# The layout of a pair of activation halves, and the rounding of buffer addresses, in a two-block transformer kernel

## The reference

```python
h = rmsnorm(x, norm_mix_g)
u = h @ w_in                                  # 1024 -> 5376
x = x + merged(rwkv(u), diff_attention(u)) @ w_out
h = rmsnorm(x, norm_mlp_g)
x = x + square(relu(h @ w_ff1)) @ w_ff2       # 1024 -> 4096 -> 1024
x = x + (p @ w_ple) * sigmoid(rmsnorm(x, norm_ple_g) @ w_ple_gate)
x = rmsnorm(x, final_norm_g)
for layer in range(2):                        # second block
    x = x + 0.5 * swiglu(rms_norm(x), ...)    # 1024 -> 2816 -> 1024
    x = x + attention(rms_norm(x)) @ w_out
    x = x + 0.5 * swiglu(rms_norm(x), ...)
```

## Time and profile before

| | before |
|---|---|
| median of 3 runs | 1467.45 us (1467.44 to 1467.86) |
| profiled execution | 1467.86 us |
| its span, first to last instruction | 1466.1 us |
| TensorE busy | 1439.1 us (98%) |
| VectorE busy | 1012.8 us (69%) |
| ScalarE busy | 767.8 us (52%) |
| granted TensorE clock | 1.00 (2.4 GHz) |
| read from HBM | 246.59 MB |

### The profile page before, as it was taken

One profiled execution on the slowest core, in us unless ns is written; L12 is line 12 of the kernel. 1 busy time (PEld: TensorE's weight loads), 2 busy tenths in 40 slices (PEclk: granted clock), 3 DMA queues, 4 the chain that ended last, 5 costly groups with the idle time before them and its releaser, 6 DMA issues.

```text
span 1466.1 us, 22896 instructions
## 1 busy us (share of the span) xinstructions
PE 1439.1 (98%) x9382; PEld 1233.7 (84%) x9382; DVE 1012.8 (69%) x1339; ACT 767.8 (52%) x1044; POOL 29.6 (2%) x96
## 2 busy tenths in 40 slices
PE   7999999999999999999999999999999999999999
PEld 6999988888887788888878888888888887788887
DVE  5785667787446787647776877468774688687753
ACT  5844365554335565435675555355553456565542
POOL 0000000000001200000000000000000000000000
PEclk9999999999999999999999999999999999999999
DMA  8441124555553465554424555545555454255552
GB/s 312 160 173 60 60 88 169 202 205 196 198 200 145 145 229 175 198 197 156 165 87 145 202 199 176 197 163 211 176 198 195 147 179 146 82 203 199 178 196 86
DMA packets 35815, 249.11 MB, mean 170 GB/s; under 512 B 4096, under 2 KB 4224, under 8 KB 6144
## 3 DMA queue, kind: packets, MB, share of 16 engines
q1 hardware_dynamic: 35712, 247.65, 47.6%
HBM read 246.59 MB, written 1.05 MB: 169 GB/s over the span
## 4 chain that ended last, share of the span: by engine, by line
PE 65%; DVE 1%; ACT 1%; issue 0%; POOL 0%; DVEq 0%; ACTq 0%; POOLq 0%
PE ps L1842 19%; PE ps L1801 10%; PE ps L1841 9%; PE ps L1803 9%; PE ps L1802 9%; PE ps L1838 3%; PE ps L1839 1%; PE ps L2145 1%; PE ps L2125 1%; PE ps L1871 1%; PE ps L2134 0%; PE ps L2074 0%; DVE lo L2494 0%; PE ps L2107 0%; DVE X L2543 0%
## 5 line engine op out<-in xcount | busy, mean ns | idle before, releaser
L2494 DVE TENSOR_TENSOR lo<-raw,hi 128x2048 fp32r<-128x2048 f32 x230 | 526.3, 2290 | 237.0 <-ACT hi L2173 236.7
L2173 ACT CAST hi<-raw 128x2048 fp32r<-128x2048 f32 x230 | 439.1, 1910 | 241.2 <-PE ps L1803 238.1
L1842 PE MATMUL ps<-h,hi 128*128 128x512 f32 x1456 | 519.5, 396 | 0.0
L1841 PE MATMUL ps<-h,lo 128*128 128x256 f32 x1456 | 406.7, 279 | 0.8 <-DVE h L2518 0.8
L1842 PEld LDWEIGHTS ps<-h,hi 128*128 128x128 f32 x1456 | 273.3, 188 | 56.2
L1841 PEld LDWEIGHTS ps<-h,lo 128*128 128x128 f32 x1456 | 274.6, 189 | 10.6 <-DVE h L2518 1.1
L1801 PE MATMUL ps<-hi,a 128*128 128x512 f32 x584 | 230.3, 394 | 0.0
L1803 PE MATMUL ps<-hi,a 128*128 128x512 f32 x584 | 227.6, 390 | 0.0
L1802 PE MATMUL ps<-lo,a 128*128 128x512 f32 x584 | 227.4, 389 | 0.0
L2358 ACT COPY a<-ps 128x256 f32<-128x256 f32 x208 | 76.4, 373 | 204.3 <-PE ps L1842 198.9
L1801 PEld LDWEIGHTS ps<-hi,a 128*128 128x128 f32 x584 | 109.7, 188 | 23.7 <-issue 2.2
(11 more groups left out here) (328 smaller groups left out, 1590.2 us busy)
## 6 DMA issues: line engine op xcount, KB each, us to landing
raw<-ws SPq DMA_DIRECT2D x230, 1024.0 KB, 4.8
X<-xin SPq DMA_DIRECT2D x8, 256.0 KB, 6.3
const<-const SPq DMA_DIRECT2D x1, 1352.0 KB, 11.3
out<-X SPq DMA_DIRECT2D x4, 256.0 KB, 2.1
small<-small SPq DMA_DIRECT2D x1, 992.5 KB, 13.1
a<-row SPq DMA_DIRECT2D x1, 512.0 KB, 5.9
a<-pin SPq DMA_DIRECT2D x1, 256.0 KB, 5.1
const<-const SPq DMA_DIRECT2D x1, 64.0 KB, 2.3
```

The source lines that it names most:

```text
L1841: e.matmul(b2(sl)[:, 0, :], wl[:, k, a:a + 128], HH[:, k, :], start=False, stop=False)
L1842: t = e.matmul(b2(sl), wh[:, k, a:a + 128], h2[:, k, :, :], start=False, stop=k == 7)
L2173: e.copy(hi[j % NSPL][:, :], raw[j % NRAW][:, :]).then_inc(hi_ready, 1)
L2494: e.tensor_tensor(lo[j % NSPL][:, :], raw[j % NRAW][:, :], hi[j % NSPL][:, :].bitcast(F), ALU.subtract).then_inc(lo_ready, 1)
```

## The change

Four edits of layout, none of which adds, removes or moves an instruction; on every engine the sequence of instructions is the same.

- `fixed` rounds sizes up to 32 bytes instead of 64. The first buffer whose rounded size differs is small; everything behind it (st, RB, nt and the arena) begins 32 bytes lower.
- h is [128, 2, 8, 256] instead of [128, 8, 2, 256]: hi of all eight k, then lo of all eight. The views HH (hi) and HL (lo) are cut accordingly.
- The wide matmuls read hi and lo of one k as `h2[:, :, k, :]`: two runs of 256 elements, where `h2[:, k, :, :]` was one run of 512.
- selr, a constant for the forget gate, has 8 columns instead of 16, of which 8 were in use. The buffers behind it, Eb and ETb, thereby begin 64 bytes lower than before.

```diff
@@ -281,15 +281,15 @@
         def fixed(name, shape, dt=F):
             size = 4 * int(np.prod(shape[1:]))
             t = at(name, shape, dt, top[0])
-            top[0] += (size + 63) // 64 * 64
+            top[0] += (size + 31) // 32 * 32
             return t
...
-        h2 = fixed("h", [128, 8, 2, S], R)
-        HH, HL = h2[:, :, 0, :], h2[:, :, 1, :]
+        h2 = fixed("h", [128, 2, 8, S], R)
+        HH, HL = h2[:, 0, :, :], h2[:, 1, :, :]
@@ -459,7 +459,7 @@
-        selr = ta([128, 16], R)
+        selr = ta([128, 8], R)
@@ -1835,11 +1835,11 @@
                         if k == 0:
-                            e.matmul(b2(sl), wh[:, k, a:a + 128], h2[:, k, :, :], start=True, stop=False)
+                            e.matmul(b2(sl), wh[:, k, a:a + 128], h2[:, :, k, :], start=True, stop=False)
                             e.matmul(b2(sl)[:, 0, :], wl[:, k, a:a + 128], HH[:, k, :], start=False, stop=False)
                         else:
                             e.matmul(b2(sl)[:, 0, :], wl[:, k, a:a + 128], HH[:, k, :], start=False, stop=False)
-                            t = e.matmul(b2(sl), wh[:, k, a:a + 128], h2[:, k, :, :], start=False, stop=k == 7)
+                            t = e.matmul(b2(sl), wh[:, k, a:a + 128], h2[:, :, k, :], start=False, stop=k == 7)
@@ -2404,7 +2404,7 @@
-                    e.copy(selr[:, 0:8], K("sel"))
+                    e.copy(selr[:, :], K("sel"))
```

## The result

| | before | after |
|---|---|---|
| median | 1467.62 us (1467.44 to 1467.86, 4 runs) | 1477.89 us (1477.41 to 1479.41, 4 runs) |
| profiled execution | 1467.86 us | 1477.41 us |
| its span | 1466.1 us | 1475.6 us |

The ratio is 1.0072, 95% interval 1.0054 to 1.0089. Forecast were 1467.5 us and a range up to 1476.0; the time is above it.

The account below looks back on a forecast made before the run. TensorE, at 98% of the span, was taken as the bound, a stream of matmuls that wait for nobody. Profiled 1467.86 us plus four zero terms, with the median 0.41 us below, gave 1467.5 us; range 1463.0 to 1476.0.

Parts of the forecast that it names:

- the first part of term 3: Passes loading stationary activations from the arena, now 32 bytes past a multiple of 64: 0; without cover 8.8 us.
- Rival D: Moving operands in the arena at 32 past 64 cost TensorE a fetch: +5.7 us, 1473.2 us; chance 0.04.
- Term 1: Wide matmuls at L1838 and L1842: reading h as two runs instead of one adds 0 us.
- the ends of -4.2 and +22.1 us: Wide matmuls over h: all tiles in the short cadence, or the second run costing like beginning another matmul.
- Rival A: The second run leaves a gap in each of 1664 wide matmuls: +8.3 us, 1475.8 us; chance 0.14.
- The cadences: Wide tiles alternate between 2.777 and 2.817 us; this was forecast to stay.
- rivals B and C: Every wide tile takes the long cadence (+4.2 us, chance 0.06) or the short one (-4.2 us, chance 0.13).
- Term 2: Writes of h by ScalarE's L2179 and VectorE's L2518, four runs now 1 KB apart: 0, at most 0.07 us.
- Term 3, VectorE and ScalarE: Their accesses at 32 past 64, judged by L2563's 476 to 480 ns: 0; otherwise waits grow under 0.5 us.
- term 4: selr with 8 columns: the copy writes the same 8, Eb and ETb return to multiples of 64; 0.

Follow-up runs that it names:

- the third experiment: The changed kernel with only the arena's start rounded up to a multiple of 64 bytes again; 1467.38 us, ratio 1.0000 (0.9991 to 1.0009).

## Why the prediction was wrong

**The step that failed** is the first part of term 3: "Weights read from the arena ... 0", with the reason that a load has over 100 ns of cover. 584 triples at +20 ns (19 on average), 10.3 us in the trace, came from exactly there. Two things were wrong in it. The row it rested on the earlier trace rows is the duration of a load of 8 columns, and the durations of the loads tell nothing of this: those of the passes over the arena have a median of 188 ns before and 187 after. What changed is when the next matmul begins. And the cover was thought of as time in which a load may be late, while it wasn't a late load: the same 20 ns came with the load in its old place and the moving operand off. No row of the trace of before could have given the 20 ns, since there the passes have only operands in step with each other. But it held a sign that distances can depend on the relative place: w_proj_b, 64 bytes off, at 353 ns a triple beside w_proj_a at 360, under one line and one shape, which the earlier trace rows lumps together. The prediction also had the size in its hands: "without the cover, 5 ns each would be 8.8 us" is 1476.3 us, against 5.9 ns each measured. It made no rival of it, and so it got no chance and no place in the range.

**Rival D** was the right neighbourhood (operands 32 off cost TensorE), with the wrong operands: it priced 1,132 moving ones and gave 5.7 us and 0.04. The 64 triples by columns with a moving operand in the arena, of which oa's half went from in step to 32 off, did not get slower (357 ns a triple on average before, 354 after). Its sign "the starts in stages that read from the arena spread, the wide stretch keeps its tiles" is what the trace shows.

**Term 1** was right: the two-run operand costs 0, measured by itself at 1.0002 (0.9993 to 1.0011); the ends of -4.2 and +22.1 us were not reached, nor is there room in that interval for the 4.2 us of a run that counts like a matmul; L2028, though of a slower stream, had pointed the same way. Rival A, to which I gave most of the slower cases, and so the sentence that this zero was the step most likely to be wrong, were misplaced. **The cadences**: rivals B and C did not happen, wide tiles alternate as in the earlier trace rows. They do depend on the relative place, though: with h or the weights 32 bytes off, all tiles take 2.793 us. **Term 2**: L2179 has a median of 620 ns and L2518 of 692 after the change, 620 and 693 before; right. **Term 3, VectorE and ScalarE**: L2563 took 477 to 481 ns against 476 to 480; right, as is term 4, which the third experiment covers.

**The range** left out too much on the slower side: of all that addresses could do to TensorE only rival D was priced, at 0.04 and 5.7 us, because each operand was looked at by itself and its relation to the other was not.

## What to carry to other kernels

Where TensorE's stream is full, the distance between starts is what a layout change has to be read by, not durations, and every pair of stationary and moving operand that gets a new relative address is a change of its own, even by 32 bytes. For fp32r matmuls like these, keep big buffers that are multiplied with each other a multiple of 256 bytes apart when 512 columns move per load, and try both ways when 256 move. An argument of slack (the load has over 100 ns to spare) did not hold here: the loads' durations stayed and the starts moved apart all the same.

## What the runs showed of the hardware

- A stream of fp32r matmuls, each with its own load of 128 columns, starts every 226.7 ns with 512 columns and every 120 ns with 256, if the two operands' addresses are a multiple of 256 bytes apart. With 32 bytes between them it is 233.3 ns with 512 columns, whichever of the two lies lower. With 256 columns it is 116.7 ns where the moving operand h lies 32 above the weights, and 118.4 on average where oa lies 32 below them (the changed kernel). The sign differs between 512 and 256 columns, which I had not expected, and can't explain.
- Shifts of 32, 64 and 128 bytes cost the 512-column stream some 19 ns in three matmuls; 256 and 0 don't. The runs with 4 and 16 bytes, whose aL had moved by 64 more, cost 16 and 19. Shifting both operands alike, by 32 bytes, costs nothing. What in the chip has this period isn't shown by these runs. The Trainium skill's page "TensorE: Matmul & The Clock Gate", section "Step-by-step: what each phase is for", says that the two reads of TensorE go through independent ports and that loading the next weights takes no read bandwidth from the running matmul; no run here shows ports, but 20 ns that come and go with the relative address of the two operands are hard to square with reads that never touch each other.
- The relation of the two operands doesn't fix the pace of a 256-column stream alone: with 64 bytes between them three matmuls take 353 ns in one kernel and 340 in another. Why isn't shown.
- A moving operand in two runs 8 KB apart costs under 1 ns a matmul against one run, if anything (1664 matmuls, -1.0 to +1.6 us in all).
- With its operands in step a wide tile has one of two cadences, 2.777 or 2.817 us, that alternate for up to 38 tiles on end; with its operands 32 bytes off there is one, 2.793 us.
